# The three weight sums of a seven-product pair: their parts made and multiplied before those of the pair's two loaded units

## The reference, cut to what matters

```
def swiglu(x, w_gu, w_down):
    g, u = jnp.split(x @ w_gu, 2, axis=-1)
    return (jax.nn.silu(g) * u) @ w_down

h = h + 0.5 * rmsnorm(swiglu(rmsnorm(h, n_ffn1_pre), w_ffn1_gu, w_ffn1_down), n_ffn1_post)
...
h = h + 0.5 * rmsnorm(swiglu(rmsnorm(h, n_ffn2_pre), w_ffn2_gu, w_ffn2_down), n_ffn2_post)
```

## Time and profile before

| | |
|---|---|
| median of 3 runs | 2433.98 us (2432.99 to 2436.94) |
| the profiled execution's own time | 2433.06 us |
| its span in the profile | 2431.3 us |
| TensorE busy | 2410.6 us, 99% |
| VectorE busy | 1840.5 us, 76% |
| ScalarE busy | 1336.8 us, 55% |
| DMA, mean | 205 GB/s |

### The profile page before, as it was taken

One profiled execution on the slowest core, in us unless ns is written; L12 is line 12 of the kernel. 1 busy time (PEld: TensorE's weight loads), 2 busy tenths in 40 slices (PEclk: granted clock), 3 DMA queues, 4 the chain that ended last, 5 costly groups with the idle time before them and its releaser, 6 DMA issues.

```text
span 2431.3 us, 32326 instructions
## 1 busy us (share of the span) xinstructions
PE 2410.6 (99%) x10933; PEld 1998.5 (82%) x10933; DVE 1840.5 (76%) x2219; ACT 1336.8 (55%) x1613; POOL 440.0 (18%) x867
## 2 busy tenths in 40 slices
PE   8999999999999999999999999999999999999998
PEld 7888888888888888888888888888888888888886
DVE  6999999987566456677676464465689999998885
ACT  6555555554555556657575444444655555555553
POOL 5211212201222003223242020010112121121000
PEclk9999999999999999999999999999999999999999
DMA  7777767767778765555665677676667777676665
GB/s 243 213 215 214 221 207 218 213 208 223 226 240 257 199 188 157 170 160 159 170 183 159 200 208 195 211 238 191 209 207 220 211 215 217 208 223 211 197 204 193
DMA packets 306063, 498.53 MB, mean 205 GB/s; under 512 B 28460, under 2 KB 102320, under 8 KB 305200
## 3 DMA queue, kind: packets, MB, share of 16 engines
q1 hardware_dynamic: 282336, 457.85, 62.7%
q0 software_dynamic: 23344, 38.95, 5.0%
q10 hardware_dynamic: 288, 0.52, 0.1%
HBM read 471.39 MB, written 8.52 MB: 197 GB/s over the span
## 4 chain that ended last, share of the span: by engine, by line
PE 92%; POOL 2%; DMA 2%; DVE 2%; SPq 1%; issue 1%; ACT 0%; DVEq 0%; POOLq 0%; ACTq 0%
PE acc L770 40%; PE acc L858 39%; PE mix L858 9%; POOL mkh L733 1%; DMA sq<-mk_scratch 1%; POOL mkh L730 1%; PE acc L795 1%; DMA post_a<-n_ffn_post 1%; SPq L438 0%; SPq L472 0%; PE mix L1082 0%; DVE wlo L1971 0%; PE acc L813 0%; PE mix L831 0%; PE mix L1128 0%
## 5 line engine op out<-in xcount | busy, mean ns | idle before, releaser
L1289 ACT ACTIVATE whi<-raw 128x1024 fp32r<-128x1024 f32 x860 | 902.3, 1056 | 972.4 <-PE acc L770 480.0
L1823 DVE TENSOR_TENSOR wlo<-raw,whi 128x1024 fp32r<-128x1024 f32 x568 | 687.3, 1228 | 322.8 <-ACT whi L1289 312.2
L1971 DVE TENSOR_TENSOR wlo<-raw,whi 128x2048 fp32r<-128x2048 f32 x146 | 333.6, 2285 | 54.1 <-ACT whi L1289 54.1
L770 PE MATMUL acc<-whi,u_hi 128*128 128x512 f32 x896 | 356.9, 398 | 0.0
L770 PE MATMUL acc<-whi,u_lo 128*128 128x512 f32 x896 | 349.4, 390 | 0.0
L770 PE MATMUL acc<-wlo,u_hi 128*128 128x512 f32 x896 | 349.1, 390 | 0.0
L387 POOL DMA_DIRECT2D nat<-nat x416 | 203.5, 498 | 791.9 <-DVE nat L2058 649.0
L858 PE MATMUL acc<-whi,x_hi 128*128 128x512 f32 x860 | 334.7, 389 | 0.3 <-DVE nat L1926 0.3
L858 PE MATMUL acc<-wlo,x_hi 128*128 128x512 f32 x860 | 334.6, 389 | 0.0
L858 PE MATMUL acc<-whi,x_lo 128*128 128x512 f32 x860 | 334.6, 389 | 0.0
L770 PEld LDWEIGHTS acc<-whi,u_lo 128*128 128x128 f32 x896 | 168.2, 188 | 35.8
(11 more groups left out here) (476 smaller groups left out, 3848.7 us busy)
## 6 DMA issues: line engine op xcount, KB each, us to landing
raw<-w_ffn_gu SPq DMA_DIRECT2D x352, 512.0 KB
raw<-w_ffn_down SPq DMA_DIRECT2D x176, 512.0 KB
raw<-w_in SPq DMA_DIRECT2D x224, 256.0 KB
raw<-w_in SPq DMA_DIRECT2D x96, 512.0 KB
raw<-w_mem_kv SPq DMA_DIRECT2D x32, 512.0 KB
raw<-w_out SPq DMA_DIRECT2D x32, 512.0 KB
nat<-nat POOLq DMA_DIRECT2D x416, 32.0 KB, 3.5
raw<-w_in SPq DMA_DIRECT2D x64, 128.0 KB
```

The lines of the kernel that those rows point to most:

```text
L770: ins = nc.tensor.matmul(acc[:, par, t, :], x[:, k0 + k, cols], w[:, k, :], start=first and k == 0 and m == 0, stop=last and k == UK - 1 a ...
L1289: act(whi[:, l % RING], raw[:, l], ACT.Copy).then_inc(hi_ready, 1)
L1823: tt(wlo[:, l], raw[:, l], whi[:, l % RING].bitcast(fp32), ALU.subtract).then_inc(lo_ready, 1)
L1971: tt(wlo[:, g:g + 2], raw[:, g:g + 2], whi[:, g % RING:g % RING + 2].bitcast(fp32), ALU.subtract).then_inc(lo_ready, 2)
```

## The change

Three engines get another order within a pair by seven; the number of instructions that compute is the same.

- TensorE: the three products of the weight sums come first, then the two of g, then the two of u. The waits inside `side_of` move with them to the first side that is used (m = 3).
- ScalarE: `wsum_hi` is made at the pair's even step, before `whi` of g and of u, and waits for all four adds.
- VectorE: right behind the four adds it waits for `wsum_hi`, makes `wsum_lo`, and then `wlo` of g and of u.
- `first_sums` and two waits of GpSimd, which took the use of the last sums as the end of a pair, now wait for the pair's last unit.

```
                 def seven(q, s):
...
+                    pe.wait_ge(sem("sum_lo"), sevens(f, i, s, 1, 1))
+                    products(mix[:, 1, :], side_of(s, 3), total(0), first, last)
+                    products(mix[:, 2, :], side_of(s, 0), total(1), first, last)
+                    products(acc[:, 0, 1, :], x(1, BOTTOM), total(2), False, False).then_inc(sem("sum_used"), 1)
                     pe.wait_ge(lo_ready, n_of(g) + 1)
                     products(mix[:, 0, :], x(0, TOP), w(g, 0), first, last)
                     products(acc[:, 0, 0, :], x(1, TOP), w(g, 1), False, False).then_inc(unit_used, 1)
                     pe.wait_ge(lo_ready, n_of(u) + 1)
                     products(mix[:, 3, :], side_of(s, 1), w(u, 0), first, last)
                     products(acc[:, 1, 0, :], side_of(s, 2), w(u, 1), False, False).then_inc(unit_used, 1)
-                    pe.wait_ge(sem("sum_lo"), sevens(f, i, s, 1, 1))
-                    products(mix[:, 1, :], side_of(s, 3), total(0), first, last)
-                    products(mix[:, 2, :], side_of(s, 0), total(1), first, last)
-                    products(acc[:, 0, 1, :], x(1, BOTTOM), total(2), False, False).then_inc(sem("sum_used"), 1)
...
                 s = seven_at.index(q) if q in seven_at else None
-                if s is not None and j % 2:
-                    ac.wait_ge(sem("sums"), sevens(f, i, s, 4, 3))
-                split(n, per_i, j)
-                if s is not None and j % 2:
+                if s is not None and j % 2 == 0:
                     ac.wait_ge(sem("sums"), sevens(f, i, s, 4, 4))
                     act(wsum_hi[:, :, :], wsum[:, :, :], ACT.Copy).then_inc(sem("sum_hi"), 1)
+                split(n, per_i, j)
...
                 if s is not None and j % 2 == 0:
                     weight_sums(f, i, s, j, loads)
+                if s is not None and j % 2 == 0:
+                    ve.wait_ge(sem("sum_hi"), sevens(f, i, s, 1, 1))
+                    tt(wsum_lo[:, :, :], wsum[:, :, :], wsum_hi[:, :, :].bitcast(fp32), ALU.subtract).then_inc(sem("sum_lo"), 1)
                 if s is not None:
                     split(n, j)
                 elif j % 2:
                     split_pair(n, j)
-                if s is not None and j % 2:
-                    ve.wait_ge(sem("sum_hi"), sevens(f, i, s, 1, 1))
-                    tt(wsum_lo[:, :, :], wsum[:, :, :], wsum_hi[:, :, :].bitcast(fp32), ALU.subtract).then_inc(sem("sum_lo"), 1)
```

More of the change, by code:

```diff
@@ L643, in _ @@
             pl.wait_ge(sem("act_lo"), N_GU + 1)
-            pl.wait_ge(sem("sum_used"), sevens(0, N_GU, D7 - 1, 1, 1))
+            pl.wait_ge(unit_used, UB["down1"] + 2 * DOWN_AT[-1] + 2)
             for c in range(4):
@@ L749, in _ @@
                 swap_act(n)
-            pl.wait_ge(sem("sum_used"), sevens(1, N_GU + 1, D7 - 1, 1, 1))
+            pl.wait_ge(unit_used, UB["down2"] + 2 * U_F + 2 * LAST_AT[-1] + 2)
             fetch_block(2, a["n_ffn2_post"])
@@ L913, in side_of @@
                 def side_of(s, m):
-                    if s == 0 and m == 1:
+                    if s == 0 and m == 3:
                         pe.wait_ge(sem("side_lo"), f + 1)
@@ L928, in side_of @@
                 def side_of(s, m):
-                    if m == 1:
+                    if m == 3:
                         pe.wait_ge(sem("down_lo"), f * D7 + s + 1)
@@ L1983, in split_pairs, with first_sums @@
                     split_pair(n, j)
-                if s is not None and j % 2:
-                    ve.wait_ge(sem("sum_hi"), sevens(f, i, s, 1, 1))
-                    tt(wsum_lo[:, :, :], wsum[:, :, :], wsum_hi[:, :, :].bitcast(fp32), ALU.subtract).then_inc(sem("sum_lo"), 1)
-            def first_sums(f, i, s, h):
-                ve.wait_ge(sem("sum_used"), sevens(f, i, s, 1, 1))
+            def first_sums(f, i, n, h):
+                ve.wait_ge(unit_used, n)
                 ve.wait_ge(sem("first_copied"), per_chunk(f, i, 1, 1))
@@ L1999, in combine @@
                 if j == 2 * seven_last + 2:
-                    first_sums(f, i, (D7 if i is N_GU else N7) - 1, 0)
+                    first_sums(f, i, n, 0)
                 if j == 2 * count - 2:
@@ L2136, in last_tasks @@
                 if j == 2 * LAST_AT[-1] + 2:
-                    first_sums(1, i, D7 - 1, 1)
+                    first_sums(1, i, n0 + j, 1)
                 if j == 2 * LAST_AT[-1] + 3:
```

## The result

The changed kernel takes 2516.98 us (median; 2515.94 to 2517.73, 4 runs) against 2433.51 us in the same comparison: a ratio of 1.0341, 95% interval [1.0326, 1.0356]. It is 83.5 us slower; 2527 us was forecast, with 2503 to 2552 as the range. The profiled span is 2515.0 us, 83.7 us more than before.

What follows compares the result with a forecast made beforehand. TensorE was taken as the bound, VectorE in effect a second one 1.2 us behind; 78 us in `quads`, 13 in `down` and 1 in the second run of f = 1 gave 2527 us, range 2503 to 2552.

Steps and rivals of the forecast that it cites:

- The bound and the stop: TensorE bounds, VectorE 1.2 us behind; at `wsum_lo` VectorE stands still 1.55 us more at each of 78 pairs by seven.
- The wait at the end of the iteration: In `quads`, at the third pair by seven, VectorE waits about 0.9 us for `whi`, as g's slot is released later.
- Rival 1: In `quads`, VectorE's chain alone counts, without the extra `whi` wait at the iteration's end: +70 to 80, 2508 us; chance 0.12.
- The first iteration of a loop: In each `quads` loop, TensorE starts unhindered for its first pairs, so this iteration loses only about 1.4 us.
- this term, 78 us forecast: Both `quads` loops: nine iterations at 4.2 us more plus a first at 1.4 us, twice, 78 us.
- `down`: In `down`, 1.16 us more per pair by seven, 6 in each FFN: 6.6 us, twice 13 us.
- The round trip for the side sums: In `down`, VectorE's 1.72 us wait for `whi` looks like slack but is a round trip inside VectorE's own chain.
- The second run: Second run of f = 1, with pairs by seven every second pair: 0.2 us each, 1 us in all.
- TensorE's waits: In `quads` and `down` only, TensorE waits about 70 times for `wsum_lo`, 80 us together.
- rival 2: TensorE's some 60 stops bring its clock down, up to 1.0 us lost each: 2540 to 2590 us; chance 0.06.
- rival 3: SP's queue gets its slots later and the pairs' data come after VectorE wants them: +106, 2540 us; chance 0.05.
- Rival 4: Not slower if the `quads` round trip costs VectorE under 0.41 us per pair by seven: 2433 to 2434 us; chance 0.03.

Runs made afterwards that it cites:

- e8: The changed kernel, but in `quads` the third pair by seven keeps TensorE's order of before (g, u, sums): 2500.01 us, 1.0275 to the kernel before.
- e4: The changed kernel with the add in place into raw made last and `wsum_hi` made in two copies: 2457.29 us, 1.0097 to the kernel before.
- e7: e4, but in `quads` the third pair by seven keeps TensorE's order of before (g, u, sums): 2432.59 us, 0.9997 to the kernel before.
- e6: The changed kernel with add into raw last, VectorE's subtraction of g before `wsum_lo`, ScalarE's order `whi` of g, `wsum_hi`, `whi` of u: 2472.25 us.
- e1: The changed kernel with ScalarE's and VectorE's order of before, so only TensorE's order is changed: 2518.82 us, 1.0350 to the kernel before.
- e9: The kernel before, with TensorE signalling the use of g and u 9 and 6 matmuls later, all orders kept: 2442.73 us, 1.0037.
- e2: The kernel before with ScalarE's and VectorE's order of the change, TensorE keeping g, u, sums: 2604.69 us, 1.0711 to the kernel before.

## Why the prediction was right, and where it was not

The change costs what it was said to cost where it was said to: the forecast was right in its mechanism, and about 10 us high by the terms below.

**The bound and the stop** were right: 78 waits at `wsum_lo`, 123.7 us against "near 130". The stop was sized a little high. `wsum_lo` starts 4.17, 4.13 and 4.24 us after the first add (338.53 - 334.36 for the first), not 4.29, because hand-overs were shorter than the 0.11 and 0.1 us taken. ScalarE's first copy shows both:

```profile
337.01 1.49 ACT L1416 ACTIVATE wsum_hi<-wsum 128x1536 fp32r<-128x1536 f32 x1 [6.36 <-DVE wsum L1962]
```

The last add ends at 336.97, the copy runs from 337.01 to 338.50, `wsum_lo` starts at 338.53. To ScalarE it was 0.04 us three times, back to VectorE 0.03 us twice and 0.10 us once. That makes 1.43, 1.39 and 1.50 us more than the 2.74 us of before, 4.32 us per iteration instead of 4.65.

**The wait at the end of the iteration** was forecast at 0.9 us and is 0.78; e8, which removes it, gives 0.86 us per iteration back. Rival 1, which left it out, is refuted. The way through TensorE and ScalarE measured 6.4 us where 6.5 was forecast, VectorE's own work 5.6 where 5.5 was. With the start of the sums behind the transposes 0.18 us closer (344.68 to 345.90, where it was 1.40), an iteration costs 3.7 us in the first FFN and 3.6 in the second, not 4.2. The first iteration of a loop was undersized: it costs 2.4 us (45.17 - 42.80 in the first FFN), not 1.4. Together this term, 78 us forecast, measured 70.0, which is most of the error.

**`down`** was oversized too. Two first adds there, three pairs apart, after the change:

```profile
558.20 0.68 DVE L1957 TENSOR_TENSOR wsum<-raw 128x512 f32<-128x512 f32 x1
...
574.86 0.68 DVE L1957 TENSOR_TENSOR wsum<-raw 128x512 f32<-128x512 f32 x1
```

That is 16.66 us, 1.02 more than 15.64 and not 1.16, and it is paid four times in the first FFN; the first of the five distances between the six pairs grows by 0.5 us (16.66 against 504.37 - 488.18 = 16.19), and what follows the sixth sums up to the second loop by 0.2. That is 4.8 us in the first FFN, against 6.6. The round trip for the side sums stayed at 1.72 us, so it was no slack, as said. The second run cost more than the 1 us forecast: of the 7.9 us behind 2281.03, 4.4 lie between the first and the sixth sums of `down`, so 3.5 behind them.

**TensorE's waits** were fewer than forecast: 52 for `wsum_lo`, 52.0 us, instead of about 70 and 80 us. In the iteration shown, from start to start, the stops before the sums are 1.5, 1.1 and 0.1 us beyond the usual 0.23 (1.5 to 1.9 for the first two was forecast), and the one at the turn of the iteration 0.35 (0.4 was).

**The clock** (rival 2) stayed at 1.00: TensorE's stops for `wsum_lo` are at most 1.4 us. **Late loads** (rival 3) did not appear: ScalarE waits 3.4 us for `w_ffn_down`, all near the end of the program, where it waited 2.2 us before the change.

**Rival 4's condition** was no sufficient one. It said that nothing is lost if the round trip costs VectorE less than 0.41 us per pair by seven. In e4 `wsum_lo` starts 3.06, 3.02 and 3.12 us after the first add, 0.28 to 0.38 us more than before the change, and e4 is still 23 us slower. Only with the loop cut as well (e7) is the loss gone.

**What the prediction did not see** is that the stop is not the only cause. It took TensorE's order as harmless once `wsum_lo` was in time, with the slots' later release worth only the wait of 0.9 us. Undoing the stop alone (e6) leaves 39 us, undoing VectorE's order (e1) gives nothing back. There are two limits, and the longer one sets the time: VectorE's chain with its stops (44.31 us, e8) and the loop through TensorE, ScalarE and VectorE (42.77 us with e4's short stop, 43.53 with e6). In the changed kernel they lie on one path: VectorE with its three stops up to the third `wsum_lo`, and from there through TensorE's 15 matmuls and ScalarE's copies, 0.86 us longer than VectorE's own way, which is why 45.17 is more than either. Only cutting both (e7) brings the 41.49 us back. e7 is level with the kernel before (0.9997 [0.9987, 1.0007]), so TensorE, busy throughout, is again all that counts, and no order of these instructions tried here beats it.

## What to carry to other kernels

Before an instruction is moved ahead on an engine that is nearly full, look at what its input takes to come from another engine and which instructions hid that; here 1.4 us of round trip, 78 times, met 1.2 us of slack for every three. Then walk the whole loop through the rings of buffers: moving the first use of one operand earlier and the release of another later lengthens the same loop twice, and one of them alone may cost little (10 us in e9). A reorder over three engines is best tested one engine at a time: the parts (84 and 170 us, of which the clock's falls are an estimated 8 and 37) did not add up to the whole (83).

## What the runs showed of the hardware

TensorE's clock fell after some stops that were not much longer than those of the changed kernel. In e1 it stood for 2.18 us and then ran at the full clock for some five matmuls, before their distance went from 0.23 to 0.43 us, the level of the kernel's first matmuls, 1.2 GHz; the granted clock from 343.63 to 346.62 is 0.50:

```profile
342.35 0.50 PE L858 MATMUL mix<-wsum_hi,x_hi 128*128 128x512 f32 x1 [2.18 <-DVE wsum_lo L1986]
342.69 0.39 PE L858 MATMUL mix<-wsum_lo,x_hi 128*128 128x512 f32 x1
...
343.63 0.63 PE L858 MATMUL mix<-wsum_hi,side_lo 128*128 128x512 f32 x1
344.06 0.63 PE L858 MATMUL acc<-wsum_hi,x_hi 128*128 128x512 f32 x1
```

In e2, whose stops before g are 1.8 to 1.9 us in two of three pairs by seven, this happened often enough for the mean granted clock to be 0.984 (0.999 with the change, 0.996 in e1). Not every such stop was followed by a fall: in e1's trace 5 of 18 stops of about 2.2 us were, in e2's 23 of 45 stops of 1.8 us or more, while one of 1.9 us in the mixer before the change was not the earlier trace rows. Why one is and the next is not, no run here shows. A fall cost 1.6 us, seven to eight distances of 0.43 us instead of 0.23: that is the difference between e1's iterations of 44.87 and of 46.47 us. The changed kernel's stops for `wsum_lo`, 1.4 us at most, left the clock alone.
